# Turning a norm's first chunk inside the product before it, with GpSimd taking two of the weight subtractions

## The reference

```python
def first_block(...):
    h = rms_norm(x, g_mix); proj = h @ w_in
    ...                                   # convolution, stick-breaking attention, cross attention
    x = x + merged @ w_out
    h2 = rms_norm(x, g_mlp)
    x = x + jnp.square(jax.nn.relu(h2 @ w_up)) @ w_down

def hybrid_layer(x, ...):                 # twice
    proj = x @ w_in                       # forgetting attention, retention, gate
    ...
    x = layernorm(DEEPNORM_ALPHA * x + mixed @ w_out, ln1_g, ln1_b)
    hid = jnp.square(jax.nn.relu(x @ w_ff1))
    x = layernorm(DEEPNORM_ALPHA * x + hid @ w_ff2, ln2_g, ln2_b)
```

## Time and profile before

| | |
|---|---|
| median of the runs | 1263.84 us |
| profiled execution | 1263.06 us, its span 1261.3 us |
| granted TensorE clock, mean | 0.995 |
| TensorE busy | 1225.0 us (97%) |
| weight loads of TensorE | 1085.6 us (86%) |
| VectorE busy | 769.4 us (61%), of which L727 448.3 us in 196 operations of 2291 ns |
| ScalarE busy | 608.1 us (48%), of which L329 373.9 us in 196 operations of 1911 ns |
| GpSimd | 0.2 us in 4 instructions |
| DMA | 217.31 MB, 172 GB/s over the span; a half of 1 MB lands 4.8 us after its issue (median) |
| chain that ended last | TensorE 82%, VectorE 9%, DMA 4%, ScalarE 3%, issue 2% |

### The profile page before, as it was taken

The page is one execution under the profiler, slowest core; times in us unless marked ns, Lnnn a source line. Parts: engine busy times, 40 slices in busy tenths (PEclk is TensorE's granted clock), DMA queues, the critical chain, the costliest instruction groups (busy, mean ns, idle before and its releaser), DMA issues.

```text
span 1261.3 us, 18443 instructions
## 1 busy us (share of the span) xinstructions
PE 1225.0 (97%) x7568; PEld 1085.6 (86%) x7568; DVE 769.4 (61%) x851; ACT 608.1 (48%) x677; POOL 0.2 (0%) x4
## 2 busy tenths in 40 slices
PE   5999999999999999999999999999999999999997
PEld 4979998888888789999899778999989977899895
DVE  5566875674465665555456787555575578755555
ACT  4555555555454454444365445444436544545441
POOL 0000000000000000000000000000000000000000
PEclk9999999999999999999999999999999999999999
DMA  5644344444565446554353453655535345465550
GB/s 205 229 179 141 127 167 152 170 147 150 206 214 184 164 167 215 186 196 170 134 201 134 142 202 142 232 193 187 179 134 201 135 142 200 144 225 187 186 191 33
DMA packets 32957, 217.31 MB, mean 172 GB/s; under 512 B 3840, under 2 KB 5888, under 8 KB 7168
## 3 DMA queue, kind: packets, MB, share of 16 engines
q1 hardware_dynamic: 32896, 216.44, 48.2%
HBM read 215.37 MB, written 1.05 MB: 172 GB/s over the span
## 4 chain that ended last, share of the span: by engine, by line
PE 82%; DVE 9%; DMA 4%; ACT 3%; issue 2%; SPq 0%; ACTq 0%; DVEq 0%
PE gps L1293 32%; PE gps L1332 7%; PE aps L1332 7%; PE aps L1333 7%; PE aps L1338 7%; PE gps L1333 7%; PE gps L1338 7%; DMA raw<-w 4%; DVE w_lo L727 3%; ACT w_hi L329 2%; PE aps L1451 1%; DVE B L881 1%; DVE rs L871 1%; DVE B L875 1%; DVE B L825 1%
## 5 line engine op out<-in xcount | busy, mean ns | idle before, releaser
L727 DVE TENSOR_TENSOR w_lo<-raw,w_hi 128x2048 fp32r<-128x2048 f32 x196 | 448.3, 2291 | 281.9 <-ACT w_hi L329 281.2
L329 ACT ACTIVATE w_hi<-raw 128x2048 fp32r<-128x2048 f32 x196 | 373.9, 1911 | 222.2 <-DMA raw<-w 110.2
L1293 PE MATMUL gps<-R_hi,w_hi 128*128 128x256 f32 x736 | 192.5, 283 | 0.0
L1293 PE MATMUL gps<-R_hi,w_lo 128*128 128x256 f32 x736 | 192.3, 283 | 0.0
L1293 PE MATMUL gps<-H_hi,w_hi 128*128 128x256 f32 x640 | 171.1, 289 | 5.9 <-ACT H_hi L364 5.7
L1293 PE MATMUL gps<-H_hi,w_lo 128*128 128x256 f32 x640 | 167.9, 284 | 0.0
L1332 PE MATMUL aps<-w_hi,Q_hi 128*128 128x512 f32 x416 | 162.6, 391 | 1.6 <-DVE Q_lo L931 1.0
L1333 PE MATMUL aps<-w_lo,Q_hi 128*128 128x512 f32 x416 | 162.2, 390 | 0.0
L1293 PE MATMUL gps<-R_lo,w_hi 128*128 128x256 f32 x736 | 147.6, 283 | 0.0
L1293 PEld LDWEIGHTS gps<-R_hi,w_lo 128*128 128x128 f32 x736 | 141.2, 192 | 0.8
L1293 PEld LDWEIGHTS gps<-R_hi,w_hi 128*128 128x128 f32 x736 | 141.1, 192 | 0.8
(11 more groups left out here) (214 smaller groups left out, 1431.8 us busy)
## 6 DMA issues: line engine op xcount, KB each, us to landing
raw<-w SPq DMA_DIRECT2D x196, 1024.0 KB, 4.8
B<-rows SPq DMA_DIRECT2D x4, 1024.0 KB, 5.0
B<-x_t SPq DMA_DIRECT2D x2, 512.0 KB, 4.7
B<-mem_t SPq DMA_DIRECT2D x1, 1024.0 KB, 8.6
B<-x SPq DMA_DIRECT2D x1, 1024.0 KB, 7.0
B<-con SPq DMA_DIRECT2D x1, 1024.0 KB, 8.8
out<-B SPq DMA_DIRECT2D x4, 256.0 KB, 2.0
B<-rows SPq DMA_DIRECT2D x1, 512.0 KB, 6.7
```

What stands on the lines that cost most here:

```text
L329: act.activation(w_hi[:, ring(l), :], raw[:, raw_slot(l), :], ACT.Copy)\
L727: dve.tensor_tensor(w_lo[:, ring(l), :], raw[:, raw_slot(l), :], w_hi[:, ring(l), :].bitcast(F32), ALU.subtract)\
L1293: return pe.matmul(gps[:, bank_, nt * T:(nt + 1) * T], w[:, r, c:c + P], op[:, k, :], start=start, stop=stop, skip_group_check=True)
```

## The change

On TensorE `turn` now handles one chunk, and `tokens_part` can do one between its eight high products and its four low ones. The first chunk of a norm is turned inside the last part of the product before it; the other three inside the first three parts of the product behind it. ScalarE and VectorE take the chunks one by one in the matching order: in the MLP norm ScalarE squares between them, and in a layer norm VectorE makes the second chunk's low part inside `rooted(1)`.

GpSimd gets an instruction stream with the same subtraction as L727: the third up half of the first FFN, and in each layer of the second model the second and third up half. ScalarE rounds the third up half amid the norm (in the MLP norm after the second root, in a layer norm between the first and the second chunk) and no longer at the start of the FFN. VectorE's subtraction of the first up half moves between the two low parts of the retention. In the FFN both engines handle the sixth half after the squares' results, and VectorE waits for GpSimd's subtraction before its own of the fourth half.

```diff
@@ ScalarE
             def mlp_norm():
...
+                squared(0, 0)
+                squared(0, 1)
+                root_start(0, 0)
+                turn_hi(N_MLP, 0, R_hi)
+                squared(1, 0)
+                turn_hi(N_MLP, 1, R_hi)
+                squared(1, 1)
+                root_start(0, 1)
+                split(0, FFN1 + 2)
+                turn_hi(N_MLP, 2, R_hi)
+                turn_hi(N_MLP, 3, R_hi)
+
+            def layer_norm(n, hi, following=None):
 
                 for m in range(2):
                     root_start(1 + n, m)
                     if hi is not None:
-                        turn_hi(N_LN + n, m, hi)
+                        turn_hi(N_LN + n, 2 * m, hi)
+                        if m == 0 and following is not None:
+                            split(*following)
+                        turn_hi(N_LN + n, 2 * m + 1, hi)
...
             def ffn(h0, l0, n):
 
                 ub = 16 * n
-                split(h0, l0 + 2)
                 split(h0, l0 + 3)
                 up_relu(h0, l0, ub, 0)
                 up_relu(h0, l0, ub, 1)
                 split(h0, l0 + 4)
-                split(h0, l0 + 5)
                 up_hi(n, ub, 0)
                 up_hi(n, ub, 1)
+                split(h0, l0 + 5)
...
                             act.activation(operand(Q_hi, m, 1), four(retention_turned(m)), ACT.Copy)\
                                .then_inc(s["gn_hi"], 1)
-                        split(g0, p + LFFN)
-                        split(g0, p + LFFN + 1)
-                layer_norm(ly * 2, R_hi)
+                            split(g0, p + LFFN + m)
+                layer_norm(ly * 2, R_hi, (g0, p + LFFN + 2))
@@ VectorE
                 added(1, 0)
                 turn_lo(N_MLP, 0, R_hi, R_lo)
                 added(1, 1)
+                turn_lo(N_MLP, 1, R_hi, R_lo)
                 rooted(1)
-                turn_lo(N_MLP, 1, R_hi, R_lo)
+                turn_lo(N_MLP, 2, R_hi, R_lo)
+                turn_lo(N_MLP, 3, R_hi, R_lo)
...
                     finished(m, 0)
+                    if m and hi is not None:
+                        turn_lo(i, 1, hi, lo)
                     centred(m, 1)
...
             def ffn(h0, l0, n):
                 ub = 16 * n
-                split(h0, l0 + 2)
+                dve.wait_ge(s["lo_ready"], h0 + (l0 + 3))
                 split(h0, l0 + 3)
                 up_square(ub, 0)
                 up_square(ub, 1)
                 split(h0, l0 + 4)
-                split(h0, l0 + 5)
                 up_lo(ub, 0)
                 up_lo(ub, 1)
+                split(h0, l0 + 5)
...
                 split(g0, p + LWO + 3)
                 gn_lo(0)
+                split(g0, p + LFFN)
                 gn_lo(1)
-                split(g0, p + LFFN)
-                split(g0, p + LFFN + 1)
@@ GpSimd, new
+        @block.gpsimd
+        def _(pool):
+
+            def split(h0, l):
+
+                pool.wait_ge(s["lo_ready"], h0 + l)
+                pool.wait_ge(s["hi_ready"], h0 + (l + 1))
+                pool.tensor_tensor(w_lo[:, ring(l), :], raw[:, raw_slot(l), :],
+                                   w_hi[:, ring(l), :].bitcast(F32), ALU.subtract)\
+                    .then_inc(s["lo_ready"], 1)
+
+            split(0, FFN1 + 2)
+            for ly in range(LAYERS):
+                p = 2 * ly
+                g0 = ly * HALVES2 + HALVES1 - p
+                split(g0, p + LFFN + 1)
+                split(g0, p + LFFN + 2)
@@ TensorE
                     pe.matmul(out, x, w_hi[:, r, c], start=(start and k == ks[0]), stop=False)
                     pe.matmul(out, x, w_lo[:, r, c], start=False, stop=False)
+                if between is not None:
+                    turn(*between)
                 if lo_ready is not None:
                     pe.wait_ge(*lo_ready)
...
                 for m in range(2):
-                    turn(n, m, src, ready, count)
                     for g in range(2):
...
                         ins = tokens_part(l + g, banks[m], m, g, op_hi, op_lo, start=(g == 0),
-                                          stop=(g == 1), hi_ready=(s["nhi"], c), lo_ready=(s["nlo"], c))
+                                          stop=(g == 1), hi_ready=(s["nhi"], c), lo_ready=(s["nlo"], c),
+                                          between=(n, i + 1, src, ready, count) if i < 3 else None)
```

More of the change, by code:

```diff
@@ L365, in rms_norm, with turn_hi @@
                        .then_inc(s["nhi"], 1)
[L367 to L372, removed]
+            def turn_hi(n, i, hi):
+                m, j = i // 2, i % 2
+                act.wait_ge(s["t_tr"], 4 * n + i + 1)
+                act.activation(operand(hi, m, j), four(turned(m, j)), ACT.Copy)\
+                   .then_inc(s["nhi"], 1)
             def root_start(i, m):
@@ L382, in mlp_norm, with squared @@
             def mlp_norm():
[L384 to L392, removed]
+                def squared(m, j):
+                    act.wait_ge(s["resid"], 2 * m + j + 1)
+                    act.activation(dump[:, j, :], chunk(X, m, j), ACT.Square, scale=1.0 / 32,
+                                   accum_out=stats[:, m, 20 + j:21 + j]).then_inc(s["t_sq"], 1)
+                squared(0, 0)
[10 more added lines that the diff above has]
+            def layer_norm(n, hi, following=None):
                 for m in range(2):
@@ L614, in _ @@
             ffn(0, FFN1, 0)
-            for m in range(2):
-                turn_hi(N_END, m, H_hi)
+            for i in range(4):
+                turn_hi(N_END, i, H_hi)
             for a in range(2):
@@ L809, in root, with turn_lo @@
                 newton(v, r0, a, r, None)
[L811 to L817, removed]
+            def turn_lo(n, i, hi, lo):
+                m, j = i // 2, i % 2
+                dve.wait_ge(s["nhi"], 4 * (n + 2) + i + 1)
+                dve.tensor_tensor(operand(lo, m, j), four(turned(m, j)),
+                                  operand(hi, m, j).bitcast(F32), ALU.subtract)\
+                   .then_inc(s["nlo"], 1)
             def residual(m, j, out, scale):
@@ L1129, in _, with ended @@
             ffn(0, FFN1, 0)
[L1130 to L1134, removed]
+            def ended(m, j):
+                sum_done(N_END, m, j, HALVES1)
+                residual(m, j, acc(m, j), None)
+            ended(0, 0)
+            ended(0, 1)
+            ended(1, 0)
+            turn_lo(N_END, 0, H_hi, H_lo)
+            ended(1, 1)
+            for i in range(1, 4):
+                turn_lo(N_END, i, H_hi, H_lo)
             for a in range(2):
@@ L1349, in tokens_half, with turn @@
                     .then_inc(s["gemm_done"], 1)
[L1351 to L1358, removed]
+            def turn(n, i, src, ready, count):
+                pe.wait_ge(ready, count + i + 1)
+                m, j = i // 2, i % 2
+                for k in range(4):
+                    ins = pe.transpose(turned(m, j)[:, k * P:(k + 1) * P],
+                                       chunk(src, m, j)[:, k * P:(k + 1) * P], ident)
+                ins.then_inc(s["t_tr"], 1)
             def turn_merged(j, m):
@@ L1385, in sum_tiles, with ffn @@
                 return ins
-            def ffn(h0, l0, n, src, ready, count):
+            def ffn(h0, l0, n, src, ready, count, after):
                 ub = 16 * n
@@ L1411, in last_down @@
                             pe.wait_ge(s["lo_ready"], h0 + (l + a + 1))
-                            ins = tokens_part(l + a, acc(m, a), m, par_, Q_hi, Q_lo, stop=True)
+                            ins = tokens_part(l + a, acc(m, a), m, par_, Q_hi, Q_lo, stop=True,
+                                              between=after if m and a else None)
                             ins.then_inc(s["acc_ready" if m == 0 else "gemm_done"], 1)
```

20 lines of the change are left out of this document (13 added, 7 removed).

## The result

| | before | after |
|---|---|---|
| median of 20 runs each, us | 1263.37 (1260.42 to 1266.0) | 1267.16 (1263.33 to 1268.35) |
| span of the profiled execution, us | 1261.3 | 1265.8 |
| mean granted clock | 0.995 | 0.994 |

What follows compares the result with a forecast made beforehand. TensorE, busy 97% of the span, was taken as the bound; only its idle time could be won. 3.05 + 3.9 + 0.4 + 0.75 - 0.3 + 1.4 = 9.2 us off 1263.84 gave 1254.6, range 1252.5 to 1267.5.

Steps and rivals of the forecast that it cites:

- layer 0, first norm: Second model, at 750 us: earlier subtraction and chunkwise turning shorten the 17.20 us stretch; gain 3.05 us.
- layer 1, first norm: Second model, at 1066 us: no idle time, so full clock, 18.04 us becomes 14.15; gain 3.9 us.
- layer 0, second norm: Second model, at 936 us, untouched by GpSimd: 14.78 us becomes 14.4; gain 0.4 us.
- end of the first FFN: At 620 us, no chain behind its additions: 14.80 us becomes 14.05; gain 0.75 us.
- MLP norm: At 437 us: TensorE waits 1.1 us for the third chunk, 14.78 us becomes 15.1; loss 0.3 us.
- FFN starts, three: First product down no longer waits for the squares' low part behind two VectorE subtractions; gain 1.4 us.
- GpSimd's three subtractions: First norms and MLP norm: about 4.6 us each, at most 6.9, hidden before TensorE wants their results.
- Rivals 1 and 2: GpSimd subtractions hold up VectorE's two-operand operations: 1264.5 us, chance 0.18; the same with clock loss, 1267.0 us, chance 0.20.
- exclusion: In the norms, GpSimd's subtraction and VectorE's two-operand operations keep each other out until the first to start ends.
- the forecast: Whole kernel: GpSimd's work hidden and all terms hold, 9.2 us gained, 1254.6 us; chance 0.47.
- the halves behind it have several us: SyncE's queue: second norm rows' load waits for a low part 1.1 us later; later halves' loads have several us.

Runs made afterwards that it cites:

- pieces: Changed kernel with each GpSimd subtraction cut into four of 512 columns, back to back; 1266.07 us, ratio 1.0014.
- earlier halves: Changed kernel with ScalarE rounding the next layer's first half between the second and third turned chunk, after the first FFN and layer 0's second norm; 1264.95 us, ratio 1.0014.
- one collision put back: all shifted, but GpSimd subtracts the third up half without waiting for the normalised chunks; 1262.81 us, ratio 0.9998.
- the version without GpSimd: Where called as fast: all shifted with every subtraction on VectorE, 1254.79 us, ratio 0.9934. Where its window is shown: no GpSimd.
- no GpSimd: Changed kernel with all GpSimd subtractions returned to VectorE, the turning inside the products kept; 1260.26 us, ratio 0.9976.
- write only: Changed kernel with GpSimd writing zeros in place of the low part, the subtraction left out; 1254.73 us, one run.
- set apart: earlier halves, with GpSimd subtracting the first up half, and the third only after all four chunks are normalised; VectorE takes the second; 1257.53 us, ratio 0.9958.
- all shifted: set apart, with layer 0's second-norm early rounding after the third turned chunk, and the MLP norm's fourth sum, square and root before the second chunk's copies; 1254.17 us, ratio 0.9931.

## Why the prediction was wrong

| Step | forecast, us gained | measured in the profiled pair |
|---|---|---|
| layer 0, first norm | 3.05 | -3.05 (17.20 to 20.25) |
| layer 1, first norm | 3.9 | -2.0 (18.04 to 20.05) |
| layer 0, second norm | 0.4 | 0.3 |
| end of the first FFN | 0.75 | 0.73 (14.80 to 14.07) |
| MLP norm | -0.3 | -0.1 (14.78 to 14.90) |
| FFN starts, three | 1.4 | 1.9 (0.3, 1.06, 0.5) |
| attention, two layers | not in the sum | -2.1 |
| sum | 9.2 | -4.3, and 0.2 lost in the start-up |

With the start-up this is the spans' difference of 4.5; the medians' is 3.8.

*The step that failed* is the one on GpSimd's three subtractions: "On their own they are hidden at any of these". They were on time for TensorE, and their length, 4.6 us, was guessed right; but they were not on their own. Their price was not their own time but VectorE's, in the chain that releases each chunk. That took the gain of both first norms and 5 us more, and with it failed what hung on it, that layer 1 has no idle time and so keeps the full clock. With the reads taken out (GpSimd only writing) both stretches are those of the forecast. In the MLP norm GpSimd starts at 444.47, when VectorE's last two-operand operation is all but over, and costs nothing.

*Rivals 1 and 2* are what happened. They put TensorE's waits at 1.7 and 3.4 us (1.60 and 3.28 measured) and the stretches, with the half clock's 1.25 each, at 20.35 and 20.25 (20.25 and 20.05). Their time, 1267.0 against 1267.16, is partly luck: the attention's 2.1 us weren't in it, the norms and the first products down came out 0.9 us better than they put them, and the kernel before, taken at 1263.84, has a median of 1263.37 over 20 runs. As a change they said 3.2 us and the medians say 3.8.
The Trainium skill had this rule (SBUF — State Buffer, Who interferes with whom), the one page that spoke against the change. The runs bear it out in three parts: a VectorE instruction with two SBUF inputs contends (2.61 and 3.39 us for 0.74), also with a one-input read (1.15), and not with a GpSimd instruction that only writes (0.74). Its 4497 ns for an addition of this size on GpSimd (GPSIMD Engine Reference, Elementwise — side-by-side cycle accounting) stands against 4.57 to 4.63 here. I gave exclusion 0.38 and the forecast 0.47 because no row of before had both engines at work. That was no evidence against a rule which says exactly what the two operations do.

*The second fault*, "the halves behind it have several us": I checked the queue of the transfers that stand beside the norms, and not ScalarE's roundings behind the last turned chunk. Turning inside the product makes the fourth chunk late by design, and what follows it in ScalarE's order moves with it. The 0.7 us won at 633 were paid back at 661, with 0.3 more. Moving one rounding won it back. How much of the half clock each run gets is open: it came behind seven of eight idle stretches of about 3.3 us (after, pieces, earlier halves, one collision put back, two each).

## What to carry to other kernels

Before work goes to GpSimd, list the VectorE operations with two SBUF operands that fall inside it; if they are in the chain that TensorE waits for, they are late until GpSimd ends, and cutting the work in pieces holds each of them once. Put it where VectorE reads PSUM or one operand, or leave it out: here the version without GpSimd was as fast. When a step is made later on purpose, follow each engine's own order behind it to the next place where TensorE asks.

## What the runs showed of the hardware

- VectorE's held L887 ended some 0.55 us after GpSimd's operation, for subtractions of 4.6 us and a copy of 1.90 us alike.
- A one-column operation with its operands in SBUF (L760) is held like a wide one: 1.25 us for 0.15.
- Four pieces of 512 columns took 5.06 us in the MLP norm, where no VectorE operation was held, and 5.48 where L887 came between two of them; one of 2048 took 4.61. GpSimd's copy of the same half took 1.90 and its write of zeros 1.81.
- The clock can fall behind less than 3.3 us of idle time, and alike idle times need not do alike. Without GpSimd it was at 0.50 from 750 to 753 in layer 0, behind a gap of 2.46 us between loads, but stayed at 1.00 in layer 1 behind one of 2.34. In the kernel before it fell in layer 1 behind gaps of 1.69 and 1.17 us, and not in layer 0 behind 1.68 and 1.17. The window of the version without GpSimd:

```profile
750.00:752.00 2.00, 2.00 (x7) 1.63 (x6) 1.93 (x4) 1.45 (x2) 0.00 (x0) 0.50 0.07 25
```

- The same code ahead of 419 us took 1.1 to 1.9 us less than in the profiled execution of before in those five executions whose clock was at 1.00 from 82 to 86 us (no GpSimd, write only, set apart, all shifted, one collision put back); in the other six, which like before were at 0.50 for a part of that time, it was within 0.3 us of it. So spans of single executions differ by that much for no edit's sake.
